# A hybrid mixer with its q/k/v steps made thinner, its 31-tap convolution shared by two engines, and its gate columns moved

## What is computed

```
proj = xn @ w_in                          # 2048 x 6160
qkv, z, b_raw, a_raw, glu = split(proj)   # columns 0:3072, 3072:4096, 4096:4104, 4104:4112, 4112:6160
qkv = silu(causal_depthwise_conv(qkv, dn_conv_w))          # 4 taps
q, k, v = split(qkv);  q, k = l2_normalize(q), l2_normalize(k)   # per head of 128
beta = sigmoid(b_raw);  g = -exp(a_log) * softplus(a_raw + dt_bias)
o = chunk_gated_delta_rule(q, k, v, g, beta)
o = rms_norm(o, dn_norm_g) * silu(z)
c = glu[:, :1024] * sigmoid(glu[:, 1024:])
c = causal_depthwise_conv(c, cf_dw_w) + cf_dw_b            # 31 taps, 1024 channels
c = silu(layer_norm(c, cf_ln_g, cf_ln_b))
return concat([o, c]) @ w_out
```

## Time and profile before

| what | us |
|---|---|
| median of 3 runs | 2729.75 |
| lowest, highest | 2729.24, 2730.69 |
| profiled execution | 2727.82 |
| its span, first to last instruction | 2726.0 |

### The profile page before, as it was taken

The page is one execution under the profiler, slowest core; times in us unless marked ns, Lnnn a source line. Parts: engine busy times, 40 slices in busy tenths (PEclk is TensorE's granted clock), DMA queues, the critical chain, the costliest instruction groups (busy, mean ns, idle before and its releaser), DMA issues. The chain is left out here.

```text
span 2726.0 us, 31318 instructions
## 1 busy us (share of the span) xinstructions
PE 2634.4 (97%) x12544; PEld 2178.3 (80%) x12544; DVE 1665.7 (61%) x2199; ACT 1257.3 (46%) x1662; POOL 0.2 (0%) x4
## 2 busy tenths in 40 slices
PE   8989999999999999998799997999999999999998
PEld 6867888888888877876678886888888888888886
DVE  6686555555555556478787876554555555555555
ACT  5554544444444446445543434444444444444443
POOL 0000000000000000000000000000000000000000
PEclk9999999999999999899999998999999999999999
DMA  6534666556655655444343335544465655565553
GB/s 215 169 115 147 222 190 193 185 186 193 192 185 187 188 190 162 129 150 138 125 154 119 131 122 193 190 158 152 161 200 185 197 186 187 188 191 191 187 190 132
DMA packets 235240, 468.69 MB, mean 172 GB/s; under 512 B 10236, under 2 KB 13015, under 8 KB 233815
## 3 DMA queue, kind: packets, MB, share of 16 engines
q1 hardware_dynamic: 235094, 466.69, 52.4%
HBM read 460.36 MB, written 6.29 MB: 171 GB/s over the span
## 5 line engine op out<-in xcount | busy, mean ns | idle before, releaser
L138 DVE TENSOR_TENSOR WL<-Wt,WH 128x1024 fp32r<-128x1024 f32 (+1 forms) x862 | 1042.2, 1211 | 794.8 <-ACT WH L135 744.2
L135 ACT ACTIVATE WH<-Wt 128x1024 fp32r<-128x1024 f32 (+1 forms) x862 | 899.1, 1047 | 851.0 <-PE ps L168 848.9
L168 PE MATMUL ps<-WH,HT 128*128 128x512 f32 (+1 forms) x3392 | 1073.4, 393 | 13.8 <-issue 13.8
L168 PE MATMUL ps<-WH,XT 128*128 128x512 f32 (+1 forms) x3392 | 1084.3, 393 | 2.4 <-DVE WL L138 2.4
L168 PEld LDWEIGHTS ps<-WH,HT 128*128 128x128 f32 x3392 | 643.5, 191 | 146.4 <-issue 15.2
L168 PEld LDWEIGHTS ps<-WH,XT 128*128 128x128 f32 x3392 | 637.0, 188 | 133.2 <-DVE WL L138 3.1
L168 PE MATMUL ps<-WL,HT 128*128 128x512 f32 (+1 forms) x1696 | 660.9, 390 | 0.0
L168 PE MATMUL ps<-WL,XT 128*128 128x512 f32 (+1 forms) x1696 | 658.7, 388 | 0.0
L168 PEld LDWEIGHTS ps<-WL,HT 128*128 128x128 f32 x1696 | 323.3, 191 | 65.5 <-issue 1.9
L168 PEld LDWEIGHTS ps<-WL,XT 128*128 128x128 f32 x1696 | 319.5, 188 | 62.4 <-issue 1.0
L138 DVE TENSOR_TENSOR H<-H,ps 128x512 f32<-128x512 f32 x144 | 92.5, 684 | 23.9 <-PE ps L168 23.8
(11 more groups left out here) (260 smaller groups left out, 1270.1 us busy)
## 6 DMA issues: line engine op xcount, KB each, us to landing
Wt<-in_mlp_w SPq DMA_DIRECT2D x128, 1024.0 KB, 5.3
Wt<-in_w_up SPq DMA_DIRECT2D x64, 1024.0 KB, 5.4
Wt<-in_w_down SPq DMA_DIRECT2D x64, 1024.0 KB, 5.0
Wt<-in_w_in SPq DMA_DIRECT2D x61, 1024.0 KB, 5.1
Wt<-in_w_out SPq DMA_DIRECT2D x32, 1024.0 KB, 5.0
Wt<-in_xa_wk SPq DMA_DIRECT2D x16, 1024.0 KB, 5.0
Wt<-in_xa_wv SPq DMA_DIRECT2D x16, 1024.0 KB, 5.1
Wt<-in_xa_wq SPq DMA_DIRECT2D x16, 1024.0 KB, 5.0
```

What stands on the lines that cost most here:

```text
L135: return self.p.act.do(lambda e: e.activation(out, in_, func, **kw), w, self.name + "_a")
L138: return self.p.dve.do(lambda e: e.tensor_tensor(out, a, b, op), w, self.name + "_v")
L168: return self.p.pe.do(lambda e: e.matmul(out, l, r, start=start, stop=stop), w, self.name + "_t" if sig else None)
```

## The change

The chunks of the mix product are taken in another order: the 16 columns are joined to z, and z with them is cut into three chunks of 336, 352 and 352 columns at the end. `line` and `in_line` are gone; `gate`, `gates` and `qkv` go straight into `bg`, so two q/k/v chunks run at a time. For that QA, QE exist twice (an arena is a fixed stretch of on-chip memory, and QA1, QE1 and PRD lie in parts free at the time). `qkv` yields after every tap and after each link of the sigmoid (`sigm_steps`, which stood in the kernel already); its first tap is now a ScalarE product. `conv31` makes, for each tap and each half of the channels, four ScalarE products into PRD (128x256, weight as the scale of a copy) and one VectorE sum over 128x1024, one group behind. `pace` sets how many empty steps follow a group: 3 until the last v chunk is out of PSUM, then 0.

```diff
-    add_gemm("mix", A["w_in_2"], (0, KT), cols(4112, 6160) + [(4096, 16)] + cols(1024, 2048) + cols(0, 1024)
-             + cols(2048, 4096))
+    add_gemm("mix", A["w_in_2"], (0, KT), cols(4112, 6160) + cols(1024, 2048) + cols(0, 1024) + cols(2048, 3072)
+             + [(3776, 336), (3072, 352), (3424, 352)])
...
-    QA = arena("QA", [P, 4, 256], 17408)
-    QE = arena("QE", [P, 4, 256], 29696)
+    QA = [arena("QA0", [P, 4, 256], 17408), arena("QA1", [P, 4, 256], 59392)]
+    QE = [arena("QE0", [P, 4, 256], 29696), arena("QE1", [P, 4, 256], 54272)]
+    PRD = [arena(f"PRD{i}", [P, 4, 256], 63488 + 4096 * i) for i in range(2)]
...
+    pace = [3]
...
-        for tb in range(2):
-            a = sigm(stm, QE2[:, tb, :], GE[:, tb, :], e[tb], free["ge"])
-            yield
-            o = GA[:, tb, c * 512:(c + 1) * 512]
-            t_ga[(c, tb)] = stm.tt(o, o, QE2[:, tb, :], MUL, a, t_ga[(c, tb)])
+        a = yield from sigm_steps(stm, QE2[:, :, :], GE[:, :, :], e, free["qe2"])
+        yield
+        o = GA[:, :, c * 512:(c + 1) * 512]
+        g = stm.tt(o, o, QE2[:, :, :], MUL, a, t_ga[(c, 0)], t_ga[(c, 1)])
...
+        def add(u, g, a):
+            cs = slice(4 * g, 4 * g + 4)
+            u_free[u] = stc.tt(AC[:, cs, :], AC[:, cs, :], PRD[u][:, :, :], ADD, a, t_conv[cs])
+            t_conv[cs] = [u_free[u]] * 4
...
         for j in range(1, 31):
-            for c in range(8):
-                t_conv[c] = stc.stt(AC[:, c, :], CP[:, c, j:j + 256], CFW[:, 8 * j + c:8 * j + c + 1], AC[:, c, :],
-                                    MUL, ADD, t_conv[c])
-                if c % 2 == 1:
+            for g in range(2):
+                u = k % 2
+                k += 1
+                a = [stc.act(PRD[u][:, i, :], CP[:, 4 * g + i, j:j + 256], ACT.Copy, t_cp, u_free[u], t_cols,
+                             scale=CFW[:, 8 * j + 4 * g + i:8 * j + 4 * g + i + 1]) for i in range(4)]
+                if left is not None:
+                    add(*left)
+                left = (u, g, a)
+                yield
+                for _ in range(pace[0]):
                     yield
+        add(*left)
...
-                    tk[i] = st.ts(QA[:, i, :], QC[:, i, 0:256], w, MUL, a, free["qa"], free["ge"], t_cols)
+                    tk[i] = st.act(A_[:, i, :], QC[:, i, 0:256], ACT.Copy, a, qa_free[u], free["ge"], t_cols, scale=w)
...
-            if j % 2:
-                yield
+            yield
...
-        a = sigm(st, qe, qa, tk, free["qe"], free["ge"], memx)
+        a = yield from sigm_steps(st, qe, qa, tk, qe_free[v], free["qe2"], memx)
...
-        if ci in (2, 3):
-            line.append(gate(ci, ci - 2))
-        if ci == 3:
-            line.append(start_conv())
-        if ci == 4:
-            line.append(gates())
+        if ci == 2:
+            bg.append(gate(2, 0))
+        if ci == 3:
+            bg.append(chain(gate(3, 1), start_conv()))
+        if ci == 9:
+            pace[0] = 0
+        if ci == 10:
+            bg.append(gates())
         if ci in qkv_at:
-            line.append(qkv(*qkv_at[ci], res))
+            bg.append(qkv(*qkv_at[ci], res, ci - 4))
...
-    bg.append(in_line())
     t_mixg = gemm("mix", ht, mix_x, ev_mix)
-    mix_open[0] = False
-    while line:
+    while not t_gt or None in tok_v:
         pump()
-    pump()
```

More of the change, by code:

```diff
@@ L1115, in build @@
     VT = arena("VT", [P, 2, 8, P], 50176)
-    Z = [arena(f"Z{i}", [P, 2, 512], 4096 * i) for i in range(2)]
+    ZZ = arena("ZZ", [P, 2, 1024], 0)
+    Z = [ZZ[:, :, 512 * i:512 * i + 512] for i in range(2)]
     XS = [inht(f"XS{i}", [P, 8, P], (i // 4) * 16384 + (i % 4) * 4096) for i in range(8)]
@@ L1211, in qkv @@
                 for i in range(4):
[L1212 to L1217, removed]
+                    t = st.tr(bk[:, i * P:(i + 1) * P], A_[:, i, tb * P:(tb + 1) * P], ident, bf, a, sig=(i == 3))
+                w = st.act(VT[:, tb, 4 * c:4 * c + 4, :].rearrange("p h d -> p (h d)"), bk, ACT.Copy, t, memx, qe_free)
+                banks.free(bi, w)
+            tok_v[c] = w
+            qa_free[u] = t
+            qe_free[v] = a
             yield
@@ L1224, in qkv @@
             t = st.mm(bk, cst("ones"), qe[:, pr * 512:(pr + 1) * 512], b, bf)
[L1225 to L1228, removed]
+            d.append(st.act(qe[:, pr * 512:(pr + 1) * 512], bk, ACT.Ln, t, bias=cst("eps")))
+            banks.free(bi, d[-1])
+        yield
+        d = st.act(qe, qe, ACT.Exp, d, scale=-0.5)
         yield
@@ L1237, in build @@
     t_pad2 = [None]
-    qkv_at = {5: ("k", 0), 6: ("k", 1), 7: ("q", 0), 8: ("q", 1), 9: ("v", 0), 10: ("v", 1)}
-    line, mix_open = [], [True]
+    qkv_at = {4: ("k", 0), 5: ("k", 1), 6: ("q", 0), 7: ("q", 1), 8: ("v", 0), 9: ("v", 1)}
     GT, t_gt = {}, []
[L1242 to L1248, removed]
     def ev_mix(ci, c0, w, acc, tok):
@@ L1306, in gates @@
         be, x, nx, gv, gl = v
-        a = st.ts(be, BA[:, :, 0:8], LOW, MAX, t_mx[4])
+        a = st.ts(be, BA[:, :, 0:8], LOW, MAX, t_ba)
+        dt = ALOG[:, 8:16].unsqueeze(1).to_broadcast([P, 2, 8])
+        b = st.tt(x, BA[:, :, 8:16], dt, ADD, t_late)
+        b = st.ts(nx, x, -1.0, MUL, b)
+        b = st.tt(nx, nx, x, MAX, b)
+        yield
         a = st.act(be, be, ACT.Exp, a, scale=-1.0)
+        b = st.act(nx, nx, ACT.Exp, b, scale=-1.0)
+        b = st.act(nx, nx, ACT.Ln, b, bias=cst("ones")[:, 0:1])
+        c = st.act(gl[:, 0, :], ALOG[:, 0:8], ACT.Exp, t_late)
+        yield
         a = st.ts(be, be, 1.0, ADD, a)
         t_be = st.recip(be, be, a)
-        dt = ALOG[:, 8:16].unsqueeze(1).to_broadcast([P, 2, 8])
-        a = st.tt(x, BA[:, :, 8:16], dt, ADD, t_late)
-        b = st.ts(nx, x, -1.0, MUL, a)
-        b = st.tt(nx, nx, x, MAX, b)
-        b = st.act(nx, nx, ACT.Exp, b, scale=-1.0)
-        b = st.act(nx, nx, ACT.Ln, b, bias=cst("ones")[:, 0:1])
-        a = st.stt(x, x, 0.0, nx, MAX, ADD, a, b)
-        b = st.act(gl[:, 0, :], ALOG[:, 0:8], ACT.Exp, t_late)
-        t_g = st.stt(gv, x, -1.0, gl[:, 0:1, :].to_broadcast([P, 2, 8]), MUL, MUL, a, b)
+        a = st.stt(x, x, 0.0, nx, MAX, ADD, b)
+        t_g = st.stt(gv, x, -1.0, gl[:, 0:1, :].to_broadcast([P, 2, 8]), MUL, MUL, a, c)
         yield
```

63 lines of the change are left out of this document (32 added, 31 removed).

## The result

The changed kernel takes 2695.93 us (median of 4 runs, 2694.07 to 2697.13) where the kernel before takes 2730.06 us beside it: a ratio of 0.9875, with a 95% interval of 0.9857 to 0.9892. It is 34.1 us faster. The forecast had 2681.0, a gain of 48.6. The direction and the range were right, the size was not, and the question is where 14.5 us went.

What follows compares the result with a forecast made beforehand. TensorE, busy 97% of the span, was taken as the bound, so savings come mainly from its waits. Mixer 38.6 + w_out_2 16.0 - xk/xv 6 = 48.6 off 2727.8 gives 2679.2, median 1.9 above: 2681, range 2665 to 2697.

Steps and rivals of the forecast that it cites:

- The wait ahead of w_out_2 and its slow restart: Ahead of w_out_2: the 13.79 us wait goes, and 2.2 lost to the lower clock; gain 16.0, other end 0.
- The waits for QE: In q/k/v chunks: waits of 4.6 us for QE replaced by four of about 2.4 for QB, 9.6 in all.
- The narrow chunks: Last three mixer chunks, 336, 352 and 352 columns: ScalarE is the bound, 67 us; 63 or 75 by product cost.
- The term for xk and xv: Key and value projections: a loss of 6 us from 27 convolution groups in xk; ends 0 and 15.
- The wide chunks: Seven 512-wide mixer chunks with transposes, sums and waits for QB: 178.1 us.
- Two marks: Signs of being right: no wait for QE or QA over 1 us; a q/k/v chunk at 26 to 28 us.
- The second: Rival: convolution products make ScalarE the bound for longer; q/k/v stalls 4.6, products 0.49, xk 15: 2707 us. Chance 0.18.
- The fourth rival: Narrow chunks and first halves of xk: clock goes to 1.2 GHz and stays, up to 146 us lost: 2827. Chance 0.05.

Runs made afterwards that it cites:

- e11: Changed kernel with pace 1 instead of 0 from the last v chunk to the end of the convolution: 2716.98 us.
- e10: Changed kernel with six empty steps ahead of the convolution's layer norm and nothing else: 2687.72 us.
- e7: Changed kernel with the regrouping of columns undone: the 16 columns a chunk of their own after the gates, z two chunks of 512: 2695.18 us.
- e2: Changed kernel with three empty steps ahead of the transposes of v: 2695.26 us.
- e6: Changed kernel with the convolution's four ScalarE products and sum per group turned back into four VectorE taps: 2710.03 us.
- e3: Changed kernel with the layer norm's two long VectorE steps cut in two each, with a step between: 2689.82 us.
- e5: Changed kernel with one empty step between the last tap of a q/k/v chunk and its sigmoid: 2685.47 us.
- e9: Changed kernel with an empty step between last tap and sigmoid, and pace 2 in the first narrow chunk alone: 2670.15 us.
- e4: Changed kernel with pace 1 in the narrow chunks until the last chunk is out of PSUM, then 0: 2684.92 us.

## Why the prediction was right, and where it was not

**Right.** The wait ahead of w_out_2 and its slow restart: 13.8 + 2.1 measured, 16.0 forecast, and e11 shows that it hangs on the place of the convolution's end. The waits for QE went, those for QB took their place at 1.7 to 3.1 us (forecast 2.4). The narrow chunks took 68.0 for a forecast of 67, with ScalarE as the bound; four products take 1.70 us, 1.6 until the next instruction follows, as assumed.

**The term for xk and xv was the worst.** I took 6 with an end of 15, and 14.1 came. The 6 were meant as the load of 27 groups. With the layer norm moved (e10) 6.4 are left, but that the two figures agree is partly luck: about half of the 6.4 is the one wait at the delta rule's start, which e7 is without under more groups. What I had not counted is the layer norm: its place was counted only as good news for w_out_2, and not as 4.96 us of VectorE work at one spot of the delta rule, and that was worth 7.7. A step that is moved has to be priced at the place where it arrives, too.

**The wide chunks** took 183.1 for a forecast of 178.1. The waits themselves were 10.9 us in the four chunks for a forecast of 9.6. More came from the clock, for which the sum had only the 0.8 us that it added to each pair of sums: of three chunks with the same 3.07 us wait the windows of the changed kernel show

```profile
1215.42:1244.70 29.28, 26.21 (x108) 20.66 (x108) 20.54 (x27) 21.74 (x32) 0.00 (x0) 0.94 0.44 144
1244.70:1275.24 30.54, 27.48 (x108) 21.81 (x108) 20.52 (x27) 21.86 (x32) 0.00 (x0) 0.89 0.42 138
```

and 28.45 at 0.94 for the third. A chunk with that wait and a clock of 1.00 took 27.7 (below), so the falls cost 1.6, 2.8 and 0.8, together 5.2. With the 1.3 of the waits that is more than the 5.0 missed; the rest of the sum for these chunks was that much too high.

**Two marks were wrong.** I expected no wait for QA above 1 us, and one of 6.25 is left. e2 shows that to cover it gains nothing as long as VectorE is as late with the next result. And I expected a q/k/v chunk at 26 to 28 us: of the four with a wait for QB one took 27.7, the others 28.4 to 30.5.

**The rivals.** The second, ScalarE as the bound for longer, was half of the truth: its loss in xk came (14.1 for its 15), its price of products (0.49) did not. But 7.7 of it were the collision, and not ScalarE. The rule of the Trainium skill (ScalarE: Activation LUTs, Rules for kernel authors) that multiplications and additions belong on VectorE spoke for that rival; the measurement decides against it here, as e6, which follows it for the convolution, is 14.1 us slower. The fourth rival, a clock that stays low, did not come: with one wait of 2.92 us for QB and four of 0.66 to 2.07 us for WL the first narrow chunk ran at 1.00, and the second at 0.84 behind the 6.25 us wait. But short waits are not always harmless. e3 has the same instructions in the first narrow chunk, and behind waits for WL of 1.37, 1.41 and 2.04 us, the last of them over at 1326.11, its clock fell to 1.2 GHz with TensorE busy again:

```profile
1307.00:1326.20 19.20, 14.38 (x90) 13.29 (x88) 13.75 (x23) 16.90 (x33) 0.00 (x0) 1.00 0.24 75
1326.30:1329.60 3.30, 3.30 (x12) 3.14 (x11) 3.30 (x4) 3.30 (x8) 0.00 (x0) 0.50 0.69 214
```

e2 has the same fall. The swinging clock of the Trainium skill (TensorE: Matmul & The Clock Gate, A second HAM failure mode: psum-queue depth-cycling) comes from such short idle times: a single fall of this kind stands in these two runs, and none in the changed kernel's. The price was small, 68.6 and 68.5 us for the narrow chunks instead of 68.0.

Not tested is the part with two chunks in flight alone. The nearest is e6, which has it without the products: 30.2 us a chunk, where the kernel before took 31 to 33.

## What to carry to other kernels

Work that is moved off the critical path is also moved to somewhere: look at each engine's queue at the new place, above all for long instructions in front of something that TensorE waits for. Where an engine stands in its queue for another one's result, put that step one slot later before moving any work: one empty step gave 10.5 us here, and where the layer norm stood decided on 8. And gains of edits that each move the same chain do not add up.

## What the runs showed of the hardware

The same wait does not always have the same price. In e7 two chunks in a row have TensorE waiting 3.07 us for QB, and only one ran with a lower clock behind it. The windows of these two chunks, and as third row that of the 16-column chunk:

```profile
1235.38:1264.70 29.32, 26.25 (x108) 20.78 (x108) 20.54 (x27) 21.84 (x32) 0.00 (x0) 0.94 0.44 143
1264.70:1292.40 27.70, 24.62 (x108) 19.53 (x108) 20.54 (x27) 21.66 (x33) 0.00 (x0) 1.00 0.46 152
...
1139.16:1161.00 21.84, 21.84 (x111) 21.16 (x111) 11.87 (x26) 12.60 (x21) 0.00 (x0) 0.58 0.57 193
```

Over all runs, q/k/v chunks with this wait took 27.7 or 28.4 to 30.6 us. Behind the waits of 1.5 us in e5 and e9 every such chunk took 25.5 to 26.2, at 1.00. e3, e4, e10 and e11 have the changed kernel's instructions up to the end of the wide chunks, and all five take 180.6 to 183.1 us for them. So differences of 2 or 3 us between kernels in this stretch say nothing of their edits.

The third row was not expected at all. The prediction said that every fall of the clock had one wait of several microseconds ahead of it. Here TensorE is counted busy for all of 21.84 us, without a wait ahead, and still ran at 1.2 GHz for most of it: what it did was matmuls of 128x16 and, with the clock already down, eight transposes. The kernel before shows it too, and the earlier trace rows were read wrongly: their 3.47 us wait begins at 1143.37, the clock was at 1.00 up to there and at 0.50 from 0.13 us later on, so the fall came right behind the 128x16 matmuls and not behind the wait:

```profile
1138.15:1143.37 5.22, 5.22 (x47) 5.13 (x46) 2.43 (x5) 4.36 (x9) 0.00 (x0) 1.00 0.58 186
1143.50:1146.84 3.34, 0.00 (x1) 0.03 (x1) 1.59 (x4) 1.70 (x5) 0.00 (x0) 0.50 0.03 11
```

That the 16 columns are the reason is not shown: no run changes their number and nothing else.
